# Differential attention in a four-layer kernel: rotary cosines on GpSimd, the head norm one head later, a fourth output tile ahead

## The reference, cut to what matters

```python
q, k, v = jnp.split(x @ w_qkv, 3, axis=-1)
q = apply_rotary(q..., cos, sin, PARTIAL_ROT)      # x*cos + swapped(x)*sin
k = apply_rotary(k..., cos, sin, PARTIAL_ROT)
lam = exp(sum(lam_q1*lam_k1)) - exp(sum(lam_q2*lam_k2)) + lambda_init
s = einsum('bhcqd,bhckd->bhcqk', qb, k) * scale    # two score maps c = 0, 1 of each head
p = masked_softmax(s, causal)
a = p[:, :, 0] - lam * p[:, :, 1]                  # the two maps are mixed
o = einsum('bhqk,bhkd->bqhd', a, v)
o = rms_norm_2(o, subln_g) * (1.0 - lambda_init)   # norm of each head's output
return o.reshape(...) @ w_o
```

## Time and profile before

| | |
|---|---|
| median of three runs | 2720.44 us |
| profiled execution | 2721.83 us |
| span of its trace | 2720.0 us |
| PE busy | 2562.3 us (94%), mean granted clock 0.977 |
| POOL busy | 1771.9 us (65%) |
| DVE busy | 1256.9 us (46%) |
| ACT busy | 778.4 us (29%) |
| DMA | 208.64 MB, mean 77 GB/s |

### The profile page before, as it was taken

One profiled execution on the slowest core, in us unless ns is written; L12 is line 12 of the kernel. 1 busy time (PEld: TensorE's weight loads), 2 busy tenths in 40 slices (PEclk: granted clock), 3 DMA queues, 4 the chain that ended last, 5 costly groups with the idle time before them and its releaser, 6 DMA issues.

```text
span 2720.0 us, 34433 instructions
## 1 busy us (share of the span) xinstructions
PE 2562.3 (94%) x12264; PEld 2144.6 (79%) x12264; DVE 1256.9 (46%) x1943; ACT 778.4 (29%) x1656; POOL 1771.9 (65%) x1596
## 2 busy tenths in 40 slices
PE   7889999999998799999998969999998999999998
PEld 6778878888887688888877757888886887788886
DVE  7967744332037543332178745333126444533312
ACT  2256642111026421110046542111004554211101
POOL 6756676666658776666676646766665656666663
PEclk9899999999999899999999979999999999999999
DMA  3210012222321022223211102222221111222222
GB/s 136 84 49 16 24 47 85 93 100 93 101 78 47 9 101 93 100 93 103 87 62 62 55 8 86 93 100 93 100 89 60 63 65 60 76 95 98 95 99 72
DMA packets 58118, 208.64 MB, mean 77 GB/s; under 512 B 6497, under 2 KB 6753, under 8 KB 58017
## 3 DMA queue, kind: packets, MB, share of 16 engines
q1 hardware_dynamic: 57744, 206.88, 22.5%
q10 hardware_dynamic: 272, 0.39, 0.1%
HBM read 205.09 MB, written 2.16 MB: 76 GB/s over the span
## 4 chain that ended last, share of the span: by engine, by line
PE 75%; DVE 14%; POOL 4%; ACT 4%; issue 2%; DMA 1%; SPq 0%; ACTq 0%; DVEq 0%; POOLq 0%
PE PS L727 22%; PE PS L728 22%; PE PS L729 22%; DVE BLK L2016 1%; POOL WL L526 1%; ACT MP L1664 1%; DVE PS L2362 1%; DVE WK L2244 1%; PE PS L760 1%; ACT GP L1454 1%; DVE GTL L2121 1%; POOL GP L638 1%; PE PS L904 1%; PE PS L1097 1%; DVE RQ L2248 1%
## 5 line engine op out<-in xcount | busy, mean ns | idle before, releaser
L727 PE MATMUL PS<-HH,WH 128*128 128x512 f32 x2304 | 920.0, 399 | 56.5 <-POOL HL L581 16.8
L526 POOL TENSOR_TENSOR WL<-raw,WH 128x1024 fp32r<-128x1024 f32 x384 | 928.9, 2419 | 32.0
L729 PE MATMUL PS<-HH,WL 128*128 128x512 f32 x2304 | 908.8, 394 | 0.0
L728 PE MATMUL PS<-HL,WH 128*128 128x512 f32 x2304 | 908.2, 394 | 0.0
L727 PEld LDWEIGHTS PS<-HH,WH 128*128 128x128 f32 x2304 | 440.3, 191 | 162.3 <-issue 32.9
L729 PEld LDWEIGHTS PS<-HH,WL 128*128 128x128 f32 x2304 | 438.8, 190 | 94.0
L728 PEld LDWEIGHTS PS<-HL,WH 128*128 128x128 f32 x2304 | 440.3, 191 | 88.1
L523 POOL TENSOR_TENSOR WH<-raw,SC 128x32 fp32r<-128x32 f32 x384 | 111.9, 291 | 544.4 <-DMA raw<-stream 501.3
L524 POOL TENSOR_SCALAR WH<-raw 128x992 fp32r<-128x992 f32 x384 | 407.7, 1062 | 0.0
L727 PE MATMUL PS<-GH,WH 128*128 (+1 forms) x704 | 273.9, 389 | 0.0
L728 PE MATMUL PS<-GL,WH 128*128 (+1 forms) x704 | 273.9, 389 | 0.0
(11 more groups left out here) (310 smaller groups left out, 3444.1 us busy)
## 6 DMA issues: line engine op xcount, KB each, us to landing
raw<-stream SPq DMA_DIRECT2D x384, 512.0 KB, 3.2
X<-x SPq DMA_DIRECT2D x4, 512.0 KB, 4.9
out<-X SPq DMA_DIRECT2D x8, 256.0 KB, 2.0
PR<-params SPq DMA_DIRECT2D x1, 536.0 KB, 6.9
RC<-consts SPq DMA_DIRECT2D x1, 256.0 KB, 8.5
RS<-consts SPq DMA_DIRECT2D x1, 256.0 KB, 8.4
WK<-positions ACTq DMA_DIRECT2D x1, 256.0 KB, 3.3
MKL<-forget_rows ACTq DMA_DIRECT2D x16, 4.0 KB
```

The costliest lines, as they stand in the source:

```text
L526: pool.tensor_tensor(WL[:, w], raw[:, w], hi.bitcast(F32), ALU.subtract).then_inc(chunk_split, 1)
L727: pe.matmul(to, h, his[k], start=start and k == 0, stop=False)
L728: pe.matmul(to, h, los[k], start=False, stop=False)
L729: last = pe.matmul(to, l, his[k], start=False, stop=stop and k == n_k - 1)
```

## The change

Four things move, all in the diff layer.

1. The cosine products of the rotation go from DVE to POOL (`cosines_k`, `cosines_q`), written straight into RQ, to which DVE then adds the sine part. ACT copies Q out before it copies the rotated K.
2. The head norm is one head later: DVE normalises head u-2 in pass u, not u-1. The square root's tile RD is doubled, the reciprocal stays in it instead of going to PSUM, and PE's values wait for the root instead of the normed output.
3. PE makes a fourth output tile in the pieces by k-tile; the `keep_busy` matmuls there go from 24 to 12, and the order of the last two passes is written anew on every engine.
4. At the start, the exponentials for lambda come ahead of the first copies of K and Q on ACT, and POOL's order of the chunks 3 to 5 has the cosines of head 0 behind chunk 3.

POOL still waits for `m_mixed` before it splits two chunks in passes 0 to 5; in pass 6 both chunks are split ahead.

```diff
-TOTALS = {"q_cos": (7, 7, 0, 0), ...
+TOTALS = {"q_cos": (7, 7, 8, 0), ...
-        RD = shaped("RD", o + 76800, [S])
+        RD = shaped("RD", o + 76800, [2, S])
@@ POOL, merged() @@
+                def cosines_k(u):
+                    pool.wait_ge(k_out[kind], u + 1)
+                    pool.tensor_tensor(RQ[:, 1], WK[:, 1], RC[:], ALU.mult).then_inc(k_cos, 1)
+                def cosines_q(u):
+                    pool.wait_ge(q_out[kind], u + 1)
+                    if u:
+                        pool.wait_ge(q_lo, before("q_lo", kind) + u)
+                    pool.tensor_tensor(RQ[:, 0], WK[:, 0], RC[:], ALU.mult).then_inc(q_cos, 1)
                 def k_rest(u, c):
                     pool.wait_ge(chunk_split, c)
+                    pool.wait_ge(q_cos, before("q_cos", kind) + u + 1)
...
-                    else:
+                else:
+                    split(c - 3, c - 2)
+                    cosines_k(0)
+                    cosines_q(0)
+                    split(c - 2, c - 1)
+                    k_rest(0, c - 1)
+                    split(c - 1, c)
+                    for u in range(7):
+                        ahead = 2 if u == 6 else 1
+                        cosines_k(u + 1)
+                        split(c, c + ahead)
+                        cosines_q(u + 1)
                         scale(u, 0)
-                        if u < 7:
-                            k_rest(u + 1, min(c + 1, last))
-                            if u:
-                                squares_rest(u - 1)
+                        k_rest(u + 1, c + ahead)
+                        if u:
+                            squares_rest(u - 1)
+                        if u < 6:
                             pool.wait_ge(m_mixed, u + 1)
-                            split(min(c + 1, last), min(c + 2, last))
-                    if kind == "fox" or u < 7:
-                        split(min(c + 2, last), min(c + 3, last))
-                    c += 3
-                if kind == "diff":
+                            split(c + 1, c + 3)
+                        c += 3
                     for t in range(3):
                         out_rest(t)
+                    split(last - 2, last - 1)
+                    out_rest(3)
+                    out_rest(4)
+                    scale(7, 0)
                     squares_rest(6)
-                    for t in range(3, 6):
-                        out_rest(t)
+                    out_rest(5)
                     split(last - 1, last)
+                    squares_rest(7)
                     out_rest(6)
-                    squares_rest(7)
                     out_rest(7)
@@ PE, values(), then the end of merged() @@
-                        pe.wait_ge(post_out, m)
+                        pe.wait_ge(post_root, m)
...
                         proj(3 * u + 5)
+                    else:
+                        out_first(q, 3, 5)
                     if u:
                         square_sums(u - 1)
-                out_first(q, 3, 6)
+                out_first(q, 5, 6)
                 turn(7, (0, 1))
                 pe.wait_ge(m_probs, before("m_probs", kind) + 48)
                 out_first(q, 0, 3, (2,))
                 turn(7, (2,))
-                out_first(q, 3, 6, (2,))
+                out_first(q, 3, 5, (2,))
                 values(7)
-                out_first(q, 6, 7, (0, 1, 2))
-                keep_busy(2, 4)
+                out_first(q, 5, 6, (2,))
+                out_first(q, 0, 5, (3,))
                 square_sums(7)
-                keep_busy(2, 20)
-                out_first(q, 7, 8, (0, 1, 2))
+                out_first(q, 5, 6, (3,))
+                out_first(q, 6, 7, (0, 1, 2, 3))
+                keep_busy(2, 12)
+                out_first(q, 7, 8, (0, 1, 2, 3))
...
-                for t in range(3, OUT_TILES):
+                for t in range(4 if q["kind"] == "diff" else 3, OUT_TILES):
@@ ACT, merged() @@
                 act.preload_act_table(ACT.Exp)
+                act.wait_ge(lam_dve, 1)
+                act.activation(SC[:, SC_LAM + 2:SC_LAM + 4], ...   (moved ahead of evac_k(0), evac_q(0))
                 def root(u):
-                    act.preload_act_table(ACT.Sqrt)
+                    if u < 7:
+                        act.preload_act_table(ACT.Sqrt)
                     act.wait_ge(post_sum, u + 1)
-                    act.activation(RD[:], PS[:, AV_BANK], ACT.Sqrt, ...
+                    if u >= 2:
+                        act.wait_ge(post_out, u - 1)
+                    act.activation(RD[:, u % 2], PS[:, AV_BANK], ACT.Sqrt, ...
@@ ACT, the loop over u @@
                     if more:
                         evac_k(u + 1)
+                    else:
+                        normed_first(0)
+                        normed_first(1)
...
+                    if not more:
+                        normed_first(2)
                     exps(2 * u, 0)
...
                     if more:
+                        evac_q(u + 1)
                         roped_k(u + 1)
-                        evac_q(u + 1)
                     else:
-                        for t in range(3):
-                            normed_first(t)
+                        root(5)
+                        act.preload_act_table(ACT.Exp)
+                        normed_first(3)
+                        normed_first(4)
...
-                        if u:
+                        if 0 < u < 6:
                             root(u - 1)
                             act.preload_act_table(ACT.Exp)
                     else:
                         root(6)
-                        for t in range(3, 6):
-                            normed_first(t)
+                        normed_first(5)
                 turned_first(7, (0, 1, 2))
-                normed_first(6)
                 whole(7)
                 act.wait_ge(m_out, before("m_out", kind) + 8)
                 square(7)
+                normed_first(6)
                 root(7)
                 normed_first(7)
@@ DVE, merged() @@
-                def rope(u, y, out_of, done):
+                def rope(u, y, out_of, cosines, start, done):
                     dve.wait_ge(out_of, u + 1)
-                    src = WK[:, y]
-                    own.sig(dve.tensor_tensor(WK[:, 3], src, RC[:], ALU.mult))
-                    own.sig(dve.stream_shuffle(WK[:, 2], src, swap8))
-                    own.wait()
+                    own.link(dve.stream_shuffle(WK[:, 2], WK[:, y], swap8))
                     own.link(dve.tensor_tensor(WK[:, 2], WK[:, 2], RS[:], ALU.mult))
-                    dve.tensor_tensor(RQ[:, y], WK[:, 3], WK[:, 2], ALU.add).then_inc(done, 1)
+                    dve.wait_ge(cosines, start + u + 1)
+                    dve.tensor_tensor(RQ[:, y], RQ[:, y], WK[:, 2], ALU.add).then_inc(done, 1)
...
                     dve.wait_ge(post_root, u + 1)
-                    dve.reciprocal(PS[:, AV_BANK], RD[:]).then_inc(post_inverse, 1)
+                    dve.reciprocal(RD[:, u % 2], RD[:, u % 2]).then_inc(post_inverse, 1)
                     dve.wait_ge(post_inverse, u + 1)
                     dve.scalar_tensor_tensor(out=O[:, u], in0=O[:, u], scalar=SC[:, SC_GAIN:SC_GAIN + 1],
-                                             in1=PS[:, AV_BANK], op0=ALU.mult, op1=ALU.mult).then_inc(post_out, 1)
+                                             in1=RD[:, u % 2], op0=ALU.mult, op1=ALU.mult).then_inc(post_out, 1)
...
                     factor(2 * u, 0, 1)
                     if more:
                         rope_q(u + 1)
+                    else:
+                        normalise(5)
...
                         rest_q(u + 1)
-                        if u:
-                            normalise(u - 1)
-                turned_rest(7, (0, 1))
+                        if u >= 2:
+                            normalise(u - 2)
+                turned_rest(7, (0, 1, 2))
                 normalise(6)
-                turned_rest(7, (2,))
                 normalise(7)
```

More of the change, by code:

```diff
@@ L360, in four_layers @@
         k_roped = {k: sem(f"k_roped_{k}") for k in LAYERS[:3]}
+        k_cos = sem("k_cos")
         k_hi = sem("k_hi")
@@ L582, in out_rest @@
                                        ).then_inc(out_lo, 1)
-                split(q["proj_chunk"] + 3, c - 1)
-                if kind == "diff":
-                    k_rest(0, c - 1)
-                split(c - 1, c)
-                for u in range(8):
-                    if kind == "fox" or u < 7:
+                if kind == "fox":
+                    split(q["proj_chunk"] + 3, c)
+                    for u in range(8):
                         split(min(c, last), min(c + 1, last))
-                    if kind == "fox":
                         if u == 7:
```

21 lines of the change are left out of this document (9 added, 12 removed).

## The result

| | before | after |
|---|---|---|
| median | 2722.01 us (4 runs, 2718.45 to 2730.4) | 2696.76 us (4 runs, 2693.45 to 2700.64) |
| profiled execution, span | 2721.83, 2720.0 us | 2693.45, 2691.7 us |
| mean granted clock of PE | 0.977 | 0.982 |

The ratio is 0.9892, with an interval of 0.9875 to 0.9909: faster by some 25 us. The forecast was 2685, its range 2673 to 2706.

What follows compares the result with a forecast made beforehand. DVE was taken to set the 28.1 us steady pass. Savings of 12 (passes 2 to 5), 5 (start) and 18.5 (end), about 36 us, took 2721.83 to 2686, median 2685; the 8-in-10 range was 2673 to 2706.

Steps and rivals of the forecast that it cites:

- Passes 2 to 5: Steady passes of the diff layer: fall from 113.05 us in all towards 24.97 each, 12 us saved, bounds 0 and 13.2.
- the one thing missing in pass 1 is the norm on DVE: Pass 1 takes 24.97 us against some 28.1 later; the only difference named was the first norm, standing at its end.
- waits inside its own order: DVE is busy 22.3 us of a 28.1 us pass; the rest are such waits, 2.89 us for ACT's copy of Q.
- The bound of 24.97 us: Length of pass 1, taken as what PE needs in a pass when nothing holds it.
- 1.1 us to spare: POOL's squares' low part ends at 17.9 us in a pass, PE's square sums come at 19.0: the tightest place.
- Rival A: POOL bounds the pass: PE waits 2 us at each square sum, passes take 27, gain 4 not 12, 2693 us; chance 0.13.
- Start: Pass 0 falls from 27.45 to about 22.4 us: 5 us saved, bounds 2 and 6.
- End: Pass 6 to tile 4: k-tile 7 about 19.7 us earlier, together 18.5 us saved, bounds 8 and 23.
- Its first link: The mix of head 6, put at 22 us after the start of pass 6.
- The wait ahead of tile 4: PE waits some 6 us before tile 4, which comes 8.7 us after k-tile 7, for POOL's split of chunk 28.
- Sum: Passes 2 to 5, start and end together: 12 + 5 + 18.5 = 35.5, about 36 us with pass 6's half-clock rows.

Runs made afterwards that it cites:

- the last version: Changed kernel with cosines back on DVE, norm one pass earlier, reciprocal of heads 0 to 4 in PSUM, one pass-6 split held behind the mix: 2686.35 us, ratio 0.9872.

## Why the prediction was right, and where it was not

**Passes 2 to 5.** Forecast 12 us saved, measured 12.1. The size was right and the reason was not, so the match is luck. The prediction said that "the one thing missing in pass 1 is the norm on DVE", counted the two cosine products off DVE, and let the wait of 2.89 us for the copy of Q go by as one among the "waits inside its own order". That wait was the cause. ACT first waited for DVE to rotate K, then copied K in four instructions, and only then copied Q, for which DVE stood waiting to rotate it. The first copy of K and the copy of Q on ACT, before:

```profile
1448.55 0.63 ACT L1637 ACTIVATE MKH<-RQ 64x512 fp32r<-64x512 f32 x1 [4.36 <-DVE RQ L2248]
...
1451.02 0.57 ACT L1624 ACTIVATE WK<-PS 128x512 f32<-128x512 f32 x1
```

Pass 1 of before has the same wait (2.89 us at 1423.64), but no norm, and can bear it (it takes 24.96 us with the swap too), which is why the norm looked like the cause. The experiments show it both ways: the swap alone brings the passes to 24.6 us, its undoing alone to 28.3, and undoing cosines and norm leaves them at 25.1. The bound of 24.97 us taken from pass 1 was also not PE's need, which is 24.0 us of work. And the lengths given for passes 3 to 5 are not from `turn_v` to `turn_v`: those are 27.33, 29.00 and 28.00 us (starts at 1490.14 and 1519.14, not 1490.90 and 1519.00). Their sum, on which the forecast rests, is the same.

**Rows against the edits.** The prediction had rows on how DVE and POOL shut each other out, but charged only 0.2 us for it, at the norm's product, and left POOL 1.1 us to spare. Rival A, PE waiting 2 us at the square sums for POOL, came true in place and in most of its size (1.31 to 1.57 us in passes 3 to 5, 2.90 in pass 1); the pass still ended at 25.2 us and not at 27, because PE's own work is shorter than I took it to be. The cosines on POOL and the reciprocal in SBUF together are what is between these 25.2 us and the 24.6 of the last version, some 0.5 of it the reciprocal (25.10 with the cosines on DVE, 24.57 with it in PSUM as well). The Trainium skill has a rule that I did not weigh and that speaks against the change (Perfetto Trace Analysis, Optimizing Scalar/DVE Operations): DVE and GpSimd share a read port into SBUF, so moving work between the two might not help. The trace agrees: K's sine product at 2.90 us instead of 0.69 cost 2.21 us more, which is more than the 1.83 us of K's cosine product that had gone.

**Start.** Forecast 5 us, measured 5.9. The cosines have no part in it (20.71 us with them on DVE), and ACT's new order in the loop has none (27.29 us in the version of before that has only that). What is left is the order at the start itself, the lambda exponentials first and POOL's order of the first chunks; no run undoes either, so that the cause of these 5.9 us is argued and not shown.

**End.** This is the term that was mis-sized: 18.5 us forecast from `turn_v(6)` to tile 4, 11.7 measured (82.2 us, 93.9 before), and 11.1 to the end of the stretch. The chain was the right one. Its first link was short: the mix of head 6 was put at t = 22 and ended at 26.6. 3.1 of these 4.6 us are its own length, since it met three subtractions of POOL and took 5.05 us instead of 1.94; from there the last turn came at 53.5 instead of 47.5, and k-tile 7 at 72.7 instead of 65. The other 3.1 of those 7.7 us gather along the chain and were not taken apart. With norm and cosines undone k-tile 7 comes at 67.0 and the mix takes 2.95 us, and with that mix held clear as well, and the reciprocal in PSUM, the last version reaches 63.3. The wait ahead of tile 4 was forecast at some 6 us and was 6.47, at 9.53 us behind k-tile 7 where 8.7 were forecast.

**Sum.** 5.9 at the start and 12.1 in passes 2 to 5, less 1.9 in pass 1, make 16 us; with the 11.1 of the end the layer's stretch fell by 27.2 us and the median by 25, against 36 forecast.

## What to carry to other kernels

A wait that stands in the rows of the bounding engine is a candidate before any of its work is: ask which instruction the releaser did first, and whether the order of two calls on it can be swapped. Where two passes differ in length, what is missing in the short one may not be the cause but only give the short one the slack to hide it. Moving DVE's work to POOL is not free even where POOL is idle, since products of two SBUF tiles and POOL's instructions shut each other out; count both engines' rows at the new place.

## What the runs showed of the hardware

- Four small mix instructions took 1.94 us with POOL standing, 5.05 beside three subtractions and 5.94 beside a subtraction and a split.
- The exclusion works the other way too: POOL's 128x992 instruction took 1.02 us, and 1.53 when DVE's product of 0.75 us with two SBUF inputs stood beside it.
- A wait of PE can cost more than its length: with the same wait of 3.12 us a pass took 27.37 us at a granted clock of 1.00, and 28.84 at 0.94.
- A DVE reciprocal of 128x512 from SBUF to SBUF took 3.35 us, to PSUM 3.36, and POOL's subtraction beside it took 2.39 and 2.36 us, where it takes 2.35 to 2.40 in other places.
